# Two-block network in one kernel: the first mixer's steps put under one written-out order, conditioning loads and two buffers moved

## The reference

```python
mod = (c_act @ w_ada[l] + b_ada[l])[:, None, :]
shift1, scale1, gate1, shift2, scale2, gate2 = jnp.split(mod, 6, axis=-1)
h = rms_norm(x, norm1_w[l]) * (1.0 + scale1) + shift1
x = x + gate1 * hybrid_mixer(h, ...)
h = rms_norm(x, norm2_w[l]) * (1.0 + scale2) + shift2
x = x + gate2 * swiglu(h, ...)
# hybrid_mixer
p = h @ w_in
qkv = silu(causal_depthwise_conv(p[..., Q_OFF:Z_OFF], conv_qkv_w))
o = gated_delta_rule_chunked(l2_normalize(q), l2_normalize(k), v, g, beta)
o = rms_norm(o, gdn_norm_w) * silu(z)
y_sc = sc_b * causal_depthwise_conv(sc_c * sc_h, conv_short_w)
return concatenate([o, y_sc]) @ w_out
```

## Time and profile before

| | |
|---|---|
| median of 3 runs | 1990.69 us (1984.79 to 1995.5) |
| the profiled execution | 1995.96 us, its span 1994.6 us |
| busy share of the span | PE 96%, PEld 82%, POOL 48%, ACT 35%, DVE 34% |
| chain that ended last, by engine | PE 85%, DVE 5%, DMA 4%, ACT 3%, issue 2%, POOL 1% |
| first mixer, first projection matmul to last of `w_out` | 44 to 409 us from the span's start |

### The profile page before, as it was taken

The page is one execution under the profiler, slowest core; times in us unless marked ns, Lnnn a source line. Parts: engine busy times, 40 slices in busy tenths (PEclk is TensorE's granted clock), DMA queues, the critical chain, the costliest instruction groups (busy, mean ns, idle before and its releaser), DMA issues.

```text
span 1994.6 us, 32732 instructions
## 1 busy us (share of the span) xinstructions
PE 1905.9 (96%) x13848; PEld 1626.1 (82%) x13848; DVE 681.3 (34%) x1066; ACT 694.9 (35%) x1054; POOL 957.1 (48%) x1262
## 2 busy tenths in 40 slices
PE   5989999999999999999999999998999899999998
PEld 4667777777888888999999999997877578888886
DVE  5665362332211010333220015665776422222101
ACT  2663221342222233322222233335665442222222
POOL 3533231535644566554555556542332455555563
PEclk9999899999999999999999999998999999999999
DMA  7333121323333222222222243210000423223231
GB/s 288 116 133 113 69 86 54 96 78 133 137 91 99 87 95 93 90 91 96 85 93 88 88 140 96 80 43 7 3 3 3 169 84 96 95 95 95 89 96 69
DMA packets 54690, 182.75 MB, mean 92 GB/s; under 512 B 6512, under 2 KB 6768, under 8 KB 54416
## 3 DMA queue, kind: packets, MB, share of 16 engines
q1 hardware_dynamic: 54544, 180.65, 27.5%
HBM read 175.39 MB, written 5.24 MB: 91 GB/s over the span
## 4 chain that ended last, share of the span: by engine, by line
PE 85%; DVE 5%; DMA 4%; ACT 3%; issue 2%; POOL 1%; SPq 0%; DVEq 0%; ACTq 0%
PE PS L543 71%; PE PS L660 4%; DMA RAWS<-w_w_in 1%; POOL WL L2259 1%; DMA ADA<-w_ada 1%; PE PS L1051 1%; PE PS L1046 1%; PE PS L1068 1%; DMA BON<-bsave 1%; PE PS L578 1%; DMA RAWS<-w_f0g 1%; PE PS L783 0%; PE PS L796 0%; PE PS L789 0%; DVE TMP L1221 0%
## 5 line engine op out<-in xcount | busy, mean ns | idle before, releaser
L2259 POOL TENSOR_TENSOR WL<-RAWS,WH 128x256 fp32r<-128x256 f32 x1074 | 821.9, 797 | 768.7 <-ACT WH L1762 768.6
L543 PE MATMUL PS<-HH,WH 128*128 128x264 f32 (+2 forms) x2184 | 669.2, 348 | 37.1 <-POOL WL L2259 9.8
L543 PE MATMUL PS<-HL,WH 128*128 128x264 f32 (+2 forms) x2184 | 654.3, 342 | 0.0
L543 PE MATMUL PS<-HH,WL 128*128 128x264 f32 (+2 forms) x2184 | 652.3, 340 | 0.0
L543 PEld LDWEIGHTS PS<-HH,WH 128*128 128x128 f32 (+1 forms) x2184 | 377.0, 190 | 103.2 <-issue 23.5
L1762 ACT ACTIVATE WH<-RAWS 128x1024 fp32r<-128x1024 f32 (+2 forms) x275 | 283.6, 1033 | 473.1 <-PE PS L543 400.4
L543 PEld LDWEIGHTS PS<-HL,WH 128*128 128x128 f32 (+1 forms) x2184 | 378.3, 190 | 48.2 <-issue 2.6
L543 PEld LDWEIGHTS PS<-HH,WL 128*128 128x128 f32 (+1 forms) x2184 | 377.5, 190 | 48.4 <-issue 0.6
L543 PE MATMUL PS<-IHf,WH 128*128 128x512 f32 (+1 forms) x704 | 209.5, 338 | 0.0
L543 PE MATMUL PS<-IHf,WL 128*128 128x512 f32 (+1 forms) x704 | 209.4, 338 | 0.0
L543 PE MATMUL PS<-ILf,WH 128*128 128x512 f32 (+1 forms) x704 | 209.3, 338 | 0.0
(11 more groups left out here) (489 smaller groups left out, 1737.7 us busy)
## 6 DMA issues: line engine op xcount, KB each, us to landing
RAWS<-w_w_in SPq DMA_DIRECT2D x52, 512.0 KB, 4.4
RAWS<-w_ada SPq DMA_DIRECT2D x32, 512.0 KB, 3.6
RAWS<-w_f0g SPq DMA_DIRECT2D x22, 512.0 KB, 3.5
RAWS<-w_f0u SPq DMA_DIRECT2D x22, 512.0 KB, 3.6
RAWS<-w_f1g SPq DMA_DIRECT2D x22, 512.0 KB, 3.5
RAWS<-w_f1u SPq DMA_DIRECT2D x22, 512.0 KB, 3.5
RAWS<-w_f2g SPq DMA_DIRECT2D x22, 512.0 KB, 3.5
RAWS<-w_f2u SPq DMA_DIRECT2D x22, 512.0 KB, 3.5
```

The lines of the kernel that those rows point to most:

```text
L543: ins = te.matmul(ps[0:m, q, o:o + b - a] if len(halves) > 1 else ps[0:m, o:o + b - a], w[:, k * m:k * m + m], v[:, k0 + k, a:b], start=fi ...
L2259: ins = ge.tensor_tensor(WL[s % NS][:, p], RAW[i % NR][:, p], WH[s % NS][:, p].bitcast(f32), ALU.subtract)
```

## The change

One list of letters, `TURNS1`, orders every engine's instructions in the rest of the first mixer (from projection 10 on). Each stream's steps have names and fixed turn numbers (`PREP1_STEPS`, `SCAN1_STEPS`, `GATE1_STEPS`); `weave`, which the second mixer used already, gives a stream its turn where its letter stands: r projections, one k-step at a turn, l the norms of q and k, p and q the even and odd pairs of chunks, s the scan, g the norm and gate, w and t and k the convolutions with their evictions and silus, x the conditioning, u and v the splits on ACT and POOL, o the split of the gated result.

On PE the list gives 32 runs of projection k-steps with chunk work between them (from the norm sums of the keys on). The two inverses of two pairs go side by side, `i6[1] i7[1] i6[0] i7[0] i8[1]` and so on, with few k-steps among them; the scan has two to three k-steps between line 783 and line 789 and after line 796. The list gives DVE the weighing of slabs 16 to 19 ahead of the first pair's `kb`, and ACT the 2048-wide silu of z ahead of the first pair's `w1`.

```diff
+TURNS1 = (
+    "wlvwllllwrlrlrlrlrllllrlrlrklrrxrtxrruwqxvpqrxqqrrprpprrptrqruxqqqqvpppprxrrrqrprrtrupqrwvrxrrwrxkrr"
...
+ADA_WITH = {_i: (2 * _i - 8, 2 * _i - 7) if _i < 21 else (_i + 13,) for _i in range(12, 27)}
+ADA_AFTER = {16: 2, 20: 3, 27: 4}
 for _i, _j in enumerate(IN_ORDER):
     ORDER += [("w_in", _j, SLAB, True)]
-    if _i < 24:
-        ORDER += [("ada", 16 + _i, SLAB, False)]
+    ORDER += [("ada", _j, SLAB, False) for _j in ADA_WITH.get(_i, ())]
...
-    BON = sbuf("BON", [128, 4, 512], st=m2)
+    BON = BK[:, :, :, :, :].rearrange("p i n a t -> p (i n a t)")[:, 0:2048]
...
 def tensor():
-        ada_column(2, main_bank("ada", 2))
-        l2_sums(4)
...
         def project_rest():
             for i in range(10, 28):
-                yield from project(IN_ORDER[i])
-                if i in (17, 25):
-                    ada_column(3 + (i == 25), main_bank("ada", 3 + (i == 25)))
-                yield
+                for k in range(8):
+                    yield 9 * (i - 10) + k
+                    if k == 0:
+                        g = project(IN_ORDER[i])
+                    next(g, None)
+                if i in ADA_AFTER:
+                    yield 9 * (i - 10) + 8
+                    ada_column(ADA_AFTER[i], main_bank("ada", ADA_AFTER[i]))
+            for k in range(4):
+                for m in range(3):
+                    yield 162 + 3 * k + m
+                    if k == 0:
+                        if m == 2:
+                            te.wait_ge(*dp[0].at("w2", 1))
+                        out2.append(slab_gemm("w_out", m, main_bank("wo", m) if m < 2 else wo_bank(m), HH, HL, KT, H1,
+                                              joined1, order=(4, 5, 6, 7, 0, 1, 2, 3)))
+                    next(out2[m])
...
                 if n:
                     te.wait_ge(*sd.at("st3", n - 1))
                     te.wait_ge(*so.at(n - 1))
-                    if c == 0:
-                        te.wait_ge(*gt_r.at("ln", b - 1))
...
                 te.wait_ge(*sd.at("vn", n))
+                if b and c == 0:
+                    te.wait_ge(*gt_r.at("ln", b - 1))
...
-            te.wait_ge(*gt_sq.at(b))
-            te.matmul(bank(6), con("ones"), RSTD[:, 0:512], start=True, stop=True).then_inc(*gt_mm.up(b))
+        def gate():
+            for b in range(4):
+                yield gate1_turn(b, "mm")
+                te.wait_ge(*gt_sq.at(b))
+                te.wait_ge(*sd.at("st3", 2 * b + 1))
+                te.matmul(bank(7), con("ones"), RSTD[:, 0:512], start=True, stop=True).then_inc(*gt_mm.up(b))
+        weave(TURNS1, r=project_rest(), l=l2_sums(4), p=prepare(0), q=prepare(1), s=scan(), g=gate())
         alternate(*out2)
-        for m in range(2, 8):
+        for m in range(3, 8):
...
 def vector():
         for i in range(1, 10):
-            ada(i + 15)
-        ada(25)
-        convolve(9)
-        modulation(2, bank(MAIN_AT["ada", 2] % 2))
-        unit_heads(4)
+        def conditioning():
+            for v in range(2, 5):
+                for k in range(8):
+                    yield 9 * (v - 2) + k
+                    ada(8 * v + k)
+                yield 9 * (v - 2) + 8
+                modulation(v, bank(MAIN_AT["ada", v] % 2))
...
 def scalar():
+        def split_ahead():
+            for i in range(18):
+                yield i
+                split_to(CUT["w_in", IN_ORDER[13]] + i)
...
 def sync():
+        for s in s_bs:
+            se.wait_ge(s, 16)
+        se.wait_ge(*rp[0].at("trk", 4))
+        se.wait_ge(*rp[1].at("trk", 3))
+        se.dma_start(BON, BSAVE).then_inc(s_bl, 16)
         se.wait_ge(*hs.at(3))
         ...
-        for s in s_bs:
-            se.wait_ge(s, 16)
-        se.dma_start(BON[:, :, :].rearrange("p k t -> p (k t)"), BSAVE).then_inc(s_bl, 16)
```

More of the change, by code:

```diff
@@ L613, in l2_sums @@
             for i in range(i0, i0 + 4):
+                yield i - i0
                 if i in (4, 5):
@@ L772, in scan @@
+        def scan():
+            for n in range(8):
+                b, c = divmod(n, 2)
+                e, t = b % 2, b // 2
+                q = HALF[c]
+                yield scan1_turn(n, "s")
                 te.wait_ge(*dp[e].at("w2", t))
@@ L1406, in scan @@
+        def scan():
+            for n in range(8):
+                b, c = divmod(n, 2)
+                e, t = b % 2, b // 2
+                q = HALF[c]
+                yield scan1_turn(n, "vn")
                 ve.wait_ge(*sp.at("s", n))
@@ L1846, in silu @@
             ae.wait_ge(*cv.at("t2", i))
+            table[0] = "silu"
             ae.activation(QKV[:, j, :], TMP[i % 3][:, 0:512], ACT.Silu).then_inc(*cv_si.up(i))
@@ L1980, in scan, with gate @@
+        def scan():
+            for n in range(8):
+                yield scan1_turn(n, "og")
                 ae.wait_ge(*sp.at("o", n))
                 ae.activation(OG[:, 0:4, 64 * n:64 * n + 64], h4(PS[:, 6, 0:256]), ACT.Copy).then_inc(*so.up(n))
-                yield
+        def gate():
             g = RSTD[:, 0:512]
-            ae.wait_ge(*so.at(2 * b + 1))
-            if b:
-                ae.wait_ge(*gt_y.at("o", b - 1))
-            ae.activation(h4(g), OG[:, 0:4, 128 * b:128 * b + 128], ACT.Square).then_inc(*gt_sq.up(b))
@@ L2000, in scalar @@
-        pr, dr = project_rest(), later_by(DELTA_TICKS, pipeline(4, prepare, scan))
-        alternate(pr, pr, dr, dr, pr, pr, dr, dr, dr)
-        for i in range(2):
-            upper_gated(i)
+            for b in range(4):
+                yield gate1_turn(b, "sq")
+                ae.wait_ge(*so.at(2 * b + 1))
+                if b:
+                    ae.wait_ge(*gt_y.at("o", b - 1))
+                ae.activation(h4(g), OG[:, 0:4, 128 * b:128 * b + 128], ACT.Square).then_inc(*gt_sq.up(b))
+                yield gate1_turn(b, "rt")
+                need_log_and_exp()
+                ae.wait_ge(*gt_mm.at(b))
+                ae.activation(g, bank(7), ACT.Ln, bias=EPSC[:, 0:1], scale=1.0 / 128).then_inc(*gt_r.up("ln", b))
+                ae.wait_ge(*gt_r.at("ln", b))
+                ae.activation(g, g, ACT.Exp, scale=-0.5).then_inc(*gt_r.up("exp", b))
@@ L2006, in scalar, with upper_gated @@
+        def upper_gated():
+            for i in range(2):
+                yield 2 * i
+                ae.wait_ge(*gt_y.at("z", (2, 3)[i]))
+                ae.wait_ge(*gemm.at(CUT["w_in", 27]))
+                ae.activation(HH[:, 0:4, NM:T2][:, :, PARTS[i]], OG[:, 0:4, PARTS[i]], ACT.Copy).then_inc(*gt_hi.up(i))
+        weave(TURNS1, u=split_ahead(), t=evictions(), k=silus(), l=l2_roots(4), p=prepare(0), q=prepare(1), s=scan(),
+              g=gate(), o=upper_gated())
         for m in range(8):
```

593 lines of the change are left out of this document (282 added, 311 removed).

## The result

The changed kernel takes 1979.07 us (median of 12 runs, 1975.79 to 1986.5) against 1992.58 us of the kernel before, run beside it on the same chip: ratio 0.9938, 95% interval 0.992 to 0.9956, some 12 us faster (13.5 by the two medians). The forecast was 20 us. Its profiled execution took 1986.24 us, 7 us above its own median, with a span of 1985.0.

A forecast was written before the change was run, and what follows sets the result against it. PE was taken as the bound but not full, busy 340.2 of 365.4 us in the first mixer. Gains of 30.3 less costs of 10.4 gave net 19.9, from median 1990.7 to about 1971 us; range 1954 to 1985.

The forecast's parts named there:

- Conditioning later: First twelve slabs: with only projection slabs in the ring, early PE waits go, 7.7 us, plus 1.7 us of half clock.
- Named steps: Chunk chain from 133 us: five PE waits for single steps get covered by other work, a gain of 7.9 us.
- handoffs: Among the reordered chunk steps: a cost of 2.0 us put back for unforeseen handoffs, between 0 and 6.
- `kb`: First pair's `kb`: DVE comes late behind convolutions, scalings and weighings, so PE waits 1.5 us, between 0 and 3.
- silu of z: On ACT ahead of the first `w1`: PE waits 1.3 us, between 0 and 3.2.
- The 2.6 us ahead of `w_out`: Wait for the split short convolution shrinks to about 1.2 us behind the last projection, a gain of 1.4.
- Three `w_out` slabs held: At `w_out` slab 3: its split starts late, PE waits 3.9 us plus 1.7 for the clock, a cost of 5.6.
- Bonus terms: Line 1727: loading `BON` early removes part of a 3.8 us wait, limited by the gate matmul; gain 2.1 us.
- Seams: From 133 us to `w_out`: 21 fewer projection runs between chunk work at 0.19 us each, a gain of 4.0 us.
- Clock: Three half-clock stretches in the mixer cost 11 us; half comes back with the waits, a gain of 5.5 us.
- The loop in the weave: Rival, chance 0.06: projection slabs from 17 on wait behind weighings and loads, 44 us more, 2015.
- The clock rule: Rival, chance 0.07: one of two stretches with both inverses side by side runs at half clock, 16 us more, 1987.

The follow-up runs named there:

- The loads alone: Kernel before with only the 24 conditioning slabs loaded after projection slabs 12 to 26, columns and weighings placed to match: 1988.68 us against 1991.77, ratio 0.9982.
- the part alone: Kernel before with only the bonus terms placed in `BK`'s space and loaded behind the last transpose: 1988.91 us, ratio 0.9986.
- the second execution: Changed kernel unaltered, run once more on the chip of other runs, against the kernel before: 1984.19 us, ratio 0.9946.
- the columns cut short: Changed kernel with conditioning columns 2, 3 and 4 computed for only the first of eight output groups: 1964.17 us, ratio 0.9874 to the kernel before.
- the spread k-steps: Changed kernel with three k-steps of projection 17 moved, on PE alone, between chunk pieces at 206 to 225 us: 1981.3 us, ratio 0.9944 to the kernel before.
- two held slabs: Changed kernel with two `w_out` slabs held ahead of the gated outputs in place of three: 1971.06 us, ratio 0.9895 to the kernel before.

## Why the prediction was right or wrong

The sign and the range hold (1979 in 1954 to 1985, 0.6% below before); the time of 1971 is 8 us too low. By the steps of the prediction:

- *Conditioning later*, 7.7 + 1.7 us: right. Projection 10 starts 9.8 us earlier, of which 1.8 are column 2, which only changed place (it stood at 124.11 for 1.84 us): 8.0 us. The loads alone give the same, 9.7 with column 2 in it. The half clock behind the wait went with it.
- *Named steps*, 7.9 us, and the costs put against it (handoffs 2.0, `kb` 1.5, silu of z 1.3): nearly right in the sum, a gain of 4.3 us where 7.9 - 4.8 = 3.1 were forecast. From projection 10 to 27 PE's idle time was 9.2 us, 7.9 of it the named waits, and all of that is gone; 4.9 us stand there now, in other shares than the 4.8: 2.4 for `kb` within its 0 to 3 (the taps took 0.78 to 1.10 us, between the two ends; with weighings 18 and 19 moved away the wait is gone), nothing for the silu of z, and 2.3 for the silu of projection 11, which no step named. The change of bank in this step is worth less than it seemed.
- *The 2.6 us ahead of `w_out`*, to 1.2: measured 1.0.
- *Three `w_out` slabs held*, 3.9 us and 1.7 for the clock: 4.0 us, and 5.9 with the clock by the run that takes the third slab away. The price was right to 0.3 us, ring and handoff as described.
- *Bonus terms*, 2.1 us: 1.4 in the trace of the part alone. The bound by the gate matmul was the wrong one: DVE's own chain ends later than it, with its steps slower while POOL works beside it.
- *Seams*, 4.0 us: there are 31 runs of projection matmuls in that window, 52 before. Busy time less half of the busy half-clock time is 212.7 - 12.0 = 200.7 us before and 210.4 - 18.8 = 191.6 after, 9 us less. The term was too small by 5, or covers things I can't tell from seams; no run takes them apart.
- *Clock*, a gain of 5.5 us and the 1.7 above: **this is the step that failed.** From projection 10 to 27, 24.0 us of PE's busy time ran at half clock before (3.4 + 9.1 + 5.9 and 5.6 of the last, up to 355.20) and 37.5 us after (3.4 + 23.9 + 6.8 + 3.4), a loss of 6.7 us in place of a gain; in the second execution it was 30.7, a loss of 3.4, and the clocks of all executions say 6 to 8 for the whole program. The reasoning was that waits bring the slow stretches and that fewer waits bring fewer. The waits went, and the longest stretch came where PE never waited. In the earlier trace rows a stretch of mostly small products at clock 1.00 told me that chunk work alone does no harm. That holds for the two inverses side by side, which run at 1.00 here as well, but not for all chunk work: the 3.4 us at 302.80 follow three scan pieces, with no wait, and no column in the 16 us ahead. What I did not look at is the column, 16 matmuls of one moving column, which stood ahead of two of the slow stretches before, those from 213.0 and 325.7 (rows below). The list puts column 2 ahead of seven chunk pieces with no projection among them.

```profile
210.62 1.84 PE L578 MATMUL PS<-KC,ACC 128*128 128x1 f32 x16
...
320.83 1.84 PE L578 MATMUL PS<-KC,ACC 128*128 128x1 f32 x16
```

- *The rivals.* The loop in the weave did not come to PE, which waits for no slab of projections 17 to 26. ACT does wait for a load there, 4.78 us until 217.08, one of the signs that were named for being wrong; but that slab is projection 18's, which PE begins at 239.73, so it cost nothing. The clock rule, at 1987, is as far above the measured time as the forecast is below, but by another mechanism. The Trainium skill (TensorE: Matmul & The Clock Gate, "A second HAM failure mode") lays such swings to short idling between groups of matmuls. The long stretch is not of that kind, since PE was busy 23.90 of 23.90 us, and with the columns cut short the clock came back although PE then idled 0.99 us more. The stretches before from 213.0 and 325.7 do have waits in them, 1.37 and 1.00 us.
- *The signs.* "More than 20 us at half clock in the mixer" came, but the kernel before has 24.0 itself, so this sign could not tell. The last projection begins 16.5 us earlier (355.20 and 338.71), where its end was to come some 25 us earlier; the waits at the eviction of slab 7 (0.6) and at `w_out` slab 3 (4.0) came as named.

With the clock at -6.7 in place of +7.2 (5.5 + 1.7), 14 us are missing from the sum of 19.9; the larger term of the seams gives back 5. That is about the 10.1 us that the first mixer and the 1.4 us that the bonus show. Without those 5 us, which nothing in the runs explains, the time would have been near 1984, at the edge of the range; that much of the range's holding is luck.

## What to carry to other kernels

When PE is the bound, a new order has to be read for what PE does in a row, not only for its waits: here a column, which loads a whole weight tile for one moving column of data, cost clock when small products or a wait followed it, and none where projection matmuls did. The granted clock by windows is the view that shows it; what it is worth in time is a question for the median. Holding one more weight slab is paid with the split that can't start, as many microseconds as that ring's turn is longer than the work left over it. On an engine that works in order, an instruction that may wait for a load belongs behind everything that PE needs next; moving four such weighings was worth some 4 us here, and moving one ahead of a state update cost 4.1.

## What the runs showed of the hardware that was not expected

Sixteen one-column matmuls (2.8 us) followed by seven pieces of small products leave TensorE at 1.2 GHz for 23.9 us without an idle moment, in two executions of one kernel alike, and for 17.1 to 23.9 in all six profiles that have this order. With two of the sixteen the products behind run at 2.4 GHz after 3.5 us. In the one place where projection matmuls stand right ahead of and right behind the sixteen, the clock stays at 1.00; column 4, ahead of a wait of 0.97 us, has 3.4 us at half clock behind it (from 347.1 in the changed kernel). A column is not needed for a short stretch: 3.4 us follow three scan pieces at 302.80. What exactly the clock follows is left open.

And less half clock in a profile did not always show in the times: the spread k-steps took 10 to 17 us of it away from projection 10 to 27 (20.4 us with them; 30.7 with two held slabs, 37.5 and 30.7 in the changed kernel's two executions), 5 to 8 us of time by half of that, and neither pair of medians tells a gain. The clock of whole executions is no higher there either: 0.981 with the spread against 0.982 and 0.981, and 0.982 against 0.985 on two held slabs.
